# Gathering second-table expert rows into an idle weight ring, with two weight chunks loaded later

## Chip, cores and metric

One core of a Trainium2 chip runs the whole program: two transformer-like blocks on 256 tokens of width 1024, in f32. The metric is the time of one execution on the device in microseconds; smaller is better.

## What is computed

The part of the first block that the change touches is the expert layer (PEER). For every token, 8 heads choose 16 experts each out of 16384 (128 = 8 x 16 per token), and each expert is one row of a table `peer_u` and one row of a table `peer_v`:

```
def expert_chunk(args):
    xc, ic, gc = args
    u = jnp.take(u_tab, ic, axis=0)
    a = jnp.einsum('chkd,cd->chk', u, xc)
    wgt = gc * jax.nn.gelu(a)
    vv = jnp.take(v_tab, ic, axis=0)
    return jnp.einsum('chk,chkd->cd', wgt, vv)
```

Ahead of it stand attention, a short convolution and the projections that give the queries and scores; behind it stands the second block: its input projection `w_in_2` (parts u, q2, k2, v, o and gates), an S5 mixer, an mLSTM mixer, and a feed-forward part.

## The kernel before

The 256 tokens are two tiles of 128 (one token for each partition). For each tile the kernel goes through 128 experts (`e` counts both tiles, 0 to 255), and each is one step on five engines:

- POOL gathers, for every token, that token's row of `peer_u` (`gather_u`, L572) and of `peer_v` (`gather_v`, L586), with an indirect DMA of 128 rows x 1024 f32, 512 KB, each. The loop issues u(e+1) and then v(e), in this order.
- DVE multiplies the u row by the token's input and sums it (`dot_expert`, L2104), into one of 16 columns `dots`. Between the dots it does pieces of the routing of later heads.
- ACT takes the GELU, multiplies by the gate, and writes a diagonal matrix of these weights, one of 8 (`weigh_expert`, L1513, L1517, L1522).
- PE multiplies the diagonal by the v row and adds it up in PSUM over a tile's 128 experts (`sum_expert`, L975: four matmul instructions for each expert). Between the sums PE does other work that is ready: queries and scores of the first block, and, in the second tile, parts u and q2 of the second block's input projection for tile 0 (sums 172 to 194).

The rows land in the buffer `gathered` (G), twelve slots of 4 KB for each partition: five for u (`NU`), seven for v (`NV`). So u(e) waits until the dot of e-5 is done (semaphore `dot_ready`), and v(e) until the sum of e-7 is done (`expert_summed`). SP loads weights in chunks of 2 MB into a ring `weight_ring` of three slots (16 KB for each partition), in the order of `CHUNKS`; `SLOT`, `BEFORE` and `LAST_USE` give a chunk's slot, the chunk that held it, and the last group of matmuls that reads that one. During the expert phase the ring's slots hold the last query weights (read by PE until experts 27 and 36), a chunk of `ada_w` (read at expert 58), and the chunks u, q2 and k2 of `w_in_2`. PE first reads u at expert 172 and q2 at expert 188; k2 is loaded when 251 sums are done. Behind the chunk q2, SP waits for the scores and for `ada` 11, issues four small loads, and waits for those 251 sums.

## Time and profile before

| | |
|---|---|
| median of 3 runs | 1431.93 us (1430.23 to 1440.47) |
| span of the profiled execution | 1439.3 us |
| PE / DVE / ACT / POOL busy | 86% / 60% / 29% / 36% of the span |
| read from HBM | 395 MB, 275 GB/s over the span |
| gathers (software queue) | 271 MB |
| chain that ended last | PE 52%, DVE 12%, POOL 11%, issue 10%, DMA 8% |
| expert phase | first gather at 174 us, last sum ends at 944 us |

"Issue" is time in which an engine waited for nothing that the profile shows. A row of the profile gives for an engine how long it was busy and what ended the idle time ahead of it. The name behind the arrow is inferred from semaphore events: where the engine named had long been done, it was another ("remote" is one that the profile could not name).

### The profile page before, as it was taken

The page shows a single profiled execution, that of the slowest core. Times are in us where ns is not written, and L with a number is a line of the kernel's source. Part 1 is how long each engine was busy: PE and PEld are TensorE (multiplying, and loading weights), DVE is VectorE, ACT ScalarE, POOL GpSimd, SP SyncE. Part 2 cuts the span into 40 slices and gives each one's busy share as a digit, 9 for nine tenths or more (in the row PEclk, how much of TensorE's full clock was granted, in tenths as well). Part 3 has the DMA queues.
Part 4 walks back from the last instruction along what each step waited for, and adds up shares of the span by engine and source line. Part 5 has one row for each costly group of instructions (what it writes and reads, how often), then busy time and mean ns, then how long its engine had stood idle before and what let it go on. Part 6 is the DMA issues. An engine that isn't in the chain of part 4 may idle for free.

```text
span 1439.3 us, 14255 instructions
## 1 busy us (share of the span) xinstructions
PE 1237.8 (86%) x4539; PEld 652.8 (45%) x4539; DVE 861.5 (60%) x1726; ACT 421.1 (29%) x1126; POOL 518.3 (36%) x578
## 2 busy tenths in 40 slices
PE   7999976989877776777698767699999999999997
PEld 2676533645322222222344222275444444899443
DVE  2445577374564565667646657728999552577445
ACT  2213242333443242342333333332212511222000
POOL 1000165555666666666666756600111200000000
PEclk9999998999999999999898999999999999999999
DMA  9896599999999999999999999934343423444440
GB/s 348 306 331 240 203 360 324 401 348 374 361 406 363 346 377 364 369 371 365 353 344 344 387 366 344 376 132 169 128 148 117 161 88 120 173 176 176 175 175 30
DMA packets 130795, 397.32 MB, mean 276 GB/s; under 512 B 10381, under 2 KB 11789, under 8 KB 130464
## 3 DMA queue, kind: packets, MB, share of 16 engines
q0 software_dynamic: 74448, 271.09, 49.9%
q1 hardware_dynamic: 54404, 120.14, 23.0%
q10 hardware_dynamic: 1868, 5.18, 1.0%
q8 instruction: 37, 0.61, 0.2%
q14 instruction: 38, 0.30, 0.1%
HBM read 395.32 MB, written 1.05 MB: 275 GB/s over the span
## 4 chain that ended last, share of the span: by engine, by line
PE 52%; DVE 12%; POOL 11%; issue 10%; DMA 8%; DVEq 3%; another core or an unknown queue 2%; ACT 2%; ACTq 0%; POOLq 0%
PE psum L663 16%; PE psum L975 14%; PE psum L1259 6%; PE psum L1298 6%; POOL gathered L572 5%; POOL gathered L586 5%; DVE work L1759 4%; DMA gathered<-in_peer_v_dram,expert_idx 4%; DVE gathered L2104 3%; DMA gathered<-in_peer_u_dram,expert_idx 3%; DVE work L2393 2%; PE psum L771 1%; DMA weight_ring<-in_w_in_dram 1%; PE psum L690 1%
## 5 line engine op out<-in xcount | busy, mean ns | idle before, releaser
L975 PE MATMUL psum<-gathered,modr 128*128 128x512 f32 x1024 | 513.5, 638 | 169.7 <-issue 71.2
L2104 DVE CUSTOM_DVE_ANT_0 gathered<-gathered,psum 128x1024 f32<-128x1024 f32 x256 | 311.4, 1217 | 203.4 <-DMA gathered<-in_peer_u_dram,expert_idx 184.8
L975 PEld LDWEIGHTS psum<-gathered,modr 128*128 128x128 f32 x1024 | 188.5, 199 | 470.1 <-issue 321.5
L572 POOL DMA_INDIRECT gathered<-in_peer_u_dram,expert_idx x256 | 243.0, 949 | 254.4 <-DVE expert_idx L1767 166.8
L586 POOL DMA_INDIRECT gathered<-in_peer_v_dram,expert_idx x256 | 244.9, 957 | 182.6 <-PE psum L975 73.1
L663 PE MATMUL psum<-weight_ring,featT 128*128 128x512 f32 x384 | 170.5, 597 | 1.7 <-ACT featT L1350 1.7
L1513 ACT ACTIVATE gel<-dots 128x1 f32<-128x1 f32 x256 | 50.9, 199 | 264.6 <-DVEq L2106 132.6
L1759 DVE TENSOR_TENSOR work<-work 128x1088 f32<-128x1088 f32 (+4 forms) x107 | 100.0, 951 | 32.8 <-ACT work L1612 18.1
L663 PEld LDWEIGHTS psum<-weight_ring,featT 128*128 128x128 f32 x384 | 71.1, 190 | 91.1 <-issue 88.9
L663 PEld LDWEIGHTS psum<-featT,weight_ring 128*128 128x128 f32 x768 | 101.7, 193 | 20.8 <-issue 14.7
L663 PE MATMUL psum<-featT,weight_ring 128*128 128x128 f32 (+2 forms) x768 | 108.3, 297 | 3.1 <-ACT featT L1350 1.5
L1522 ACT ACTIVATE modr<-ident,wgt 128x128 f32<-128x128 f32 x256 | 102.8, 402 | 22.5 <-issue 4.5
L1517 ACT ACTIVATE wgt<-gel,expert_gate 128x1 f32<-128x1 f32 x256 | 75.4, 294 | 25.0 <-issue 8.0
L608 POOL TENSOR_TENSOR gathered<-gathered,vectors 128x2048 f32<-128x2048 f32 x3 | 15.4, 5121 | 81.3 <-ACT gathered L1377 81.3
L1350 ACT COPY featT<-psum 128x512 f32<-128x512 f32 (+1 forms) x28 | 14.7, 560 | 74.1 <-PE psum L639 60.1
L602 POOL TENSOR_TENSOR gathered<-gathered,vectors 16x1024 f32<-16x1024 f32 x1 | 3.0, 3036 | 91.0 <-ACT gathered L1638 91.0
L1759 DVE TENSOR_TENSOR gathered<-gathered,psum 128x256 f32<-128x256 f32 (+1 forms) x17 | 8.7, 513 | 36.7 <-PE psum L663 31.3
L663 PE MATMUL psum<-weight_ring,uT 128*128 128x512 f32 x64 | 29.9, 622 | 0.0
L1748 ACT ACTIVATE work<-work,pack 128x256 f32<-128x256 f32 x28 | 12.7, 500 | 56.8 <-DVE work L1759 56.8
L1377 ACT COPY gathered<-psum 128x512 f32<-128x512 f32 (+1 forms) x20 | 10.2, 520 | 65.1 <-PE psum L663 57.6
L663 PE MATMUL psum<-featT,gathered 128*128 128x256 f32 x128 | 29.0, 382 | 0.0
L1759 DVE TENSOR_TENSOR vectors<-weight_ring 128x1024 f32<-128x1024 f32 x14 | 16.5, 1220 | 20.9 <-PE psum L1298 20.9
(365 smaller groups left out, 1375.0 us busy)
## 6 DMA issues: line engine op xcount, KB each, us to landing
weight_ring<-in_w_in_dram SPq DMA_DIRECT2D x13, 2048.0 KB
weight_ring<-in_ada_w_dram SPq DMA_DIRECT2D x10, 2048.0 KB
weight_ring<-in_w_up_dram SPq DMA_DIRECT2D x8, 2048.0 KB
weight_ring<-in_w_down_dram SPq DMA_DIRECT2D x8, 2048.0 KB
weight_ring<-in_peer_wq_dram SPq DMA_DIRECT2D x3, 2048.0 KB
gathered<-in_ada_w_dram SPq DMA_DIRECT2D x2, 2048.0 KB
gathered<-in_w_in_dram SPq DMA_DIRECT2D x2, 2048.0 KB
gathered<-in_peer_u_dram,expert_idx POOLq DMA_INDIRECT x256
```

The costliest lines, as they stand in the source:

```text
L572: pool.indirect_dma_start(u_rows[:, slot, :], None, T["peer_u"], bass.IndirectOffsetOnAxis(ap=expert_idx[:, r % 2, k:k + 1], axis=0),).the ...
L586: pool.indirect_dma_start(v_rows[:, slot, :], None, T["peer_v"], bass.IndirectOffsetOnAxis(ap=expert_idx[:, r % 2, k:k + 1], axis=0),).the ...
L663: last = pe.matmul(psum[0:m, bank, 0:n], lhs(k), rhs(k), start=(k == 0), stop=(k == kt - 1))
L975: mm = pe.matmul(psum[:, SUM_BANK + half, :], diag[:, e % 8, :], v_rows[:, slot, 512 * half:512 * (half + 1)], start=(e % EXPERTS == 0), s ...
L1259: last = pe.matmul(psum[:, UP_BANKS * (n % 2) + bank, at:at + P], a(g, m), b(g), start=(g == 0), stop=(g == 3))
L1298: last = pe.matmul(psum[:, PRODUCT_BANK[i], :], a(g), b(g), start=(n == 0 and g == 0), stop=(n == WINOGRAD - 1 and g == 1))
L1513: act.activation(gel[:, col:col + 1], dots[:, col:col + 1], ACT.Gelu_apprx_tanh)
L1517: act.activation(wgt[:, col:col + 1], gel[:, col:col + 1], ACT.Copy, scale=expert_gate[:, r % 2, k:k + 1])
L1522: act.activation(diag[:, e % 8, :], ident[:, :], ACT.Copy, scale=wgt[:, col:col + 1]).then_inc(flag("diag_full"), 1)
L1759: return dve.tensor_tensor(o, a, b, op)
L2104: dve.tensor_tensor_reduce(u_rows[:, slot, :], u_rows[:, slot, :], h2_rows[t], 1.0, 0.0, ALU.mult, ALU.add, dots[:, col:col + 1])
L2393: dve.tensor_tensor_scan(z[:, i, :], r, z[:, i, :], 0.0, ALU.mult, ALU.add)
```

## The change

While the ring's slots stand empty, each holds four rows of v (4 x 4 KB = 16 KB). The table `SPILL` says for which experts a slot may be used, and `place_v` gives every v row the place that has been free longest. Slot 2 takes rows of experts 62 to 245, slots 1 and 0 of experts 62 to 145 (the last that uses slot 0 is 141). So there are 19 places for v rows from expert 62, 11 from 146, and 7 or 8 from 246: v(e) then waits for the sum of e-19, and from e = 157 of e-11. The first row in each place of the ring waits for the last matmuls that read the slot's weights. SP loads chunks u and q2 only when `SPILL_DONE` sums are done (146 and 142), and the four small loads now stand ahead of them. DVE's dot of expert e also waits until ACT has done the diagonal of e-16+1, because 16 columns of `dots` would otherwise be overwritten.

```
+SPILL = {2: (62, 246), 1: (62, 146), 0: (62, 146)}
+SPILL_LAST = {2: ("turn", ("ada", 11, 0)), 1: ("group", ("wqb", 7)), 0: ("group", ("wq", 11))}
+def place_v():
+    at, before, turn = [], [], []
+    last, uses = {}, {}
+    for e in range(TT * EXPERTS):
+        open_ = list(range(NV))
+        for r in sorted(SPILL):
+            lo, hi = SPILL[r]
+            if lo <= e < hi:
+                open_ += [NV + 4 * r + j for j in range(4)]
+        slot = min(open_, key=lambda k: (last.get(k, -1), k))
+        at.append(slot)
+        before.append(last.get(slot))
+        turn.append(uses.get(slot, 0))
+        last[slot], uses[slot] = e, uses.get(slot, 0) + 1
+    return at, before, turn
+V_AT, V_BEFORE, V_TURN = place_v()
+SPILL_DONE = {r: 1 + max(e for e in range(TT * EXPERTS) if (V_AT[e] - NV) // 4 == r) for r in SPILL}
...
-                if c == LAST_ADA + 3:
+                if c == LAST_ADA + 1:
                     turn_read_wait(sp, "sc", TT - 1, 3)
                     group_wait(sp, "ada", 11)
...
+                if c in (LAST_ADA + 1, LAST_ADA + 2):
+                    sp.wait_ge(flag("expert_summed"), SPILL_DONE[SLOT[c]])
+                if c == LAST_ADA + 3:
                     sp.wait_ge(flag("expert_summed"), TT * EXPERTS - LATE_LOAD)
...
-                r, k, slot = e // ROUTE, e % ROUTE, e % NV
-                if e >= NV:
-                    pool.wait_ge(flag("expert_summed"), e - NV + 1)
+                r, k, slot = e // ROUTE, e % ROUTE, V_AT[e]
+                if V_BEFORE[e] is not None:
+                    pool.wait_ge(flag("expert_summed"), V_BEFORE[e] + 1)
+                elif slot >= NV:
+                    kind, last = SPILL_LAST[(slot - NV) // 4]
+                    if kind == "turn":
+                        turn_wait(pool, *last)
+                    else:
+                        group_wait(pool, *last)
...
-                slot = e % NV
-                pe.wait_ge(v_full[slot], 16 * (e // NV + 1))
+                pe.wait_ge(v_full[V_AT[e]], 16 * (V_TURN[e] + 1))
...
+                if e >= TOPK:
+                    dve.wait_ge(flag("diag_full"), e - TOPK + 1)
```

On POOL's queue, around v62 (L586 is `gather_v` before, L627 after). Before:

```order
148 L586 DMA gathered<-in_peer_v_dram,expert_idx 128x1024 [waits expert_summed]
149 L572 DMA gathered<-in_peer_u_dram,expert_idx 128x1024 [waits dot_ready]
150 L586 DMA gathered<-in_peer_v_dram,expert_idx 128x1024 [waits expert_summed]
151 L572 DMA gathered<-in_peer_u_dram,expert_idx 128x1024 [waits dot_ready,idx_ready]
152 L586 DMA gathered<-in_peer_v_dram,expert_idx 128x1024 [waits expert_summed]
```

And after:

```order
148 L627 DMA gathered<-in_peer_v_dram,expert_idx 128x1024 [waits expert_summed]
149 L607 DMA gathered<-in_peer_u_dram,expert_idx 128x1024 [waits dot_ready]
150 L627 DMA weight_ring<-in_peer_v_dram,expert_idx 128x1024 [waits bank_full1]
151 L607 DMA gathered<-in_peer_u_dram,expert_idx 128x1024 [waits dot_ready,idx_ready]
152 L627 DMA weight_ring<-in_peer_v_dram,expert_idx 128x1024 [waits bank_full1]
```

The order of the gathers is the same; from v62 they go to the ring, and the first twelve there wait for groups of matmuls in place of sums.

On SP's queue, behind the last query weights (L513 is the load of a chunk before, L548 after; `w_in` rows are chunks u, q2 and k2 of the second block). Before:

```order
27 L513 DMA weight_ring<-in_ada_w_dram 128x8x512 [waits bank_full1]
28 L513 DMA weight_ring<-in_w_in_dram 128x8x512 [waits bank_full1] x2
29 L506 DMA vectors<-in_ln_g_dram 1x1024 [waits bank_full1,turn_read,turned]
30 L506 DMA vectors<-in_ln_b_dram 1x1024
31 L508 DMA work<-in_meta_tokens_dram 16x1024
32 L509 DMA work<-in_s_bc_dram 128x1024
33 L513 DMA weight_ring<-in_w_in_dram 128x8x512 [waits expert_summed]
34 L513 DMA weight_ring<-in_w_in_dram 128x8x512 [waits bank_full1]
```

And after:

```order
27 L548 DMA weight_ring<-in_ada_w_dram 128x8x512 [waits bank_full1]
28 L538 DMA vectors<-in_ln_g_dram 1x1024 [waits bank_full1,turn_read]
29 L538 DMA vectors<-in_ln_b_dram 1x1024
30 L540 DMA work<-in_meta_tokens_dram 16x1024
31 L541 DMA work<-in_s_bc_dram 128x1024
32 L548 DMA weight_ring<-in_w_in_dram 128x8x512 [waits expert_summed]
33 L548 DMA weight_ring<-in_w_in_dram 128x8x512 [waits expert_summed,bank_full1]
34 L548 DMA weight_ring<-in_w_in_dram 128x8x512 [waits expert_summed,turned]
```

The two chunks moved from ahead of the four small loads to behind them, and all three chunks now wait for sums.

## Rows read from the trace of the kernel before

**Rows 1.** The page's slices of the span: GB/s moved, 36 us each.
```profile
GB/s 348 306 331 240 203 360 324 401 348 374 361 406 363 346 377 364 369 371 365 353 344 344 387 366 344 376 132 169 128 148 117 161 88 120 173 176 176 175 175 30
```

**Rows 2.** Busy time by stretch: PE, PEld, DVE, ACT, POOL, clock, DMA share, GB/s.
```profile
372.00:925.00 553.00, 415.66 (x951) 163.11 (x949) 345.17 (x808) 200.71 (x623) 363.78 (x382) 0.94 0.96 366
...
540.00:558.00 18.00, 13.88 (x28) 4.74 (x28) 8.72 (x15) 6.29 (x21) 10.44 (x12) 1.00 1.02 408
558.00:562.00 4.00, 1.98 (x4) 0.68 (x4) 1.48 (x4) 1.80 (x6) 2.86 (x4) 1.00 0.60 185
...
613.00:643.00 30.00, 21.70 (x44) 7.89 (x42) 20.26 (x38) 10.42 (x34) 20.79 (x21) 0.94 0.97 362
```

**Rows 3.** Groups by line, 375 to 925 us: busy, mean ns | idle before, releasers.
```profile
L2104 DVE CUSTOM_DVE_ANT_0 gathered<-gathered,psum 128x1024 f32<-128x1024 f32 x192 | 233.7, 1217 | 140.2 <-DMA gathered<-in_peer_u_dram,expert_idx 123.3 <-issue 16.3
L586 POOL DMA_INDIRECT gathered<-in_peer_v_dram,expert_idx x190 | 182.3, 960 | 122.9 <-issue 47.4 <-PE psum L975 40.5 <-remote 34.9
L572 POOL DMA_INDIRECT gathered<-in_peer_u_dram,expert_idx x190 | 180.4, 950 | 66.0 <-issue 58.1 <-DVEq L2106 8.0
```

**Rows 4.** POOL's waits, 375 to 613 us: us in total, times, longest.
```profile
POOL gathered L586 <- PE psum L975: 16.0, 7, 4.4
POOL gathered L572 <- DVEq L2106: 7.7, 7, 2.8
POOL gathered L586 <- remote: 7.0, 2, 4.4
```

**Rows 5.** The same, 613 to 911 us.
```profile
POOL gathered L586 <- PE psum L975: 24.5, 16, 3.0
POOL gathered L586 <- remote: 24.1, 10, 4.8
```

**Rows 6.** POOL's timeline, six v gathers; then matmuls of L975 until 722.9 us.
```profile
723.14 0.94 POOL L586 DMA_INDIRECT gathered<-in_peer_v_dram,expert_idx  x1 [1.43 <-PE psum L975]
...
726.82 0.94 POOL L586 DMA_INDIRECT gathered<-in_peer_v_dram,expert_idx  x1 [1.50 <-PE psum L975]
...
732.22 0.94 POOL L586 DMA_INDIRECT gathered<-in_peer_v_dram,expert_idx  x1 [0.74 <-issue]
...
770.65 0.94 POOL L586 DMA_INDIRECT gathered<-in_peer_v_dram,expert_idx  x1 [1.49 <-PE psum L975]
...
774.38 0.94 POOL L586 DMA_INDIRECT gathered<-in_peer_v_dram,expert_idx  x1 [1.55 <-PE psum L975]
...
780.32 0.94 POOL L586 DMA_INDIRECT gathered<-in_peer_v_dram,expert_idx  x1 [1.28 <-PE psum L975]
...
190.00:722.90 532.90, 353.74 (x708) 129.65 (x708) 0.94 0.97 366
```

**Rows 7.** POOL's timeline: v82, v94, u127 and v126 (start, duration, idle before).
```profile
432.12 1.33 POOL L586 DMA_INDIRECT gathered<-in_peer_v_dram,expert_idx  x1 [4.11 <-PE psum L975]
...
466.41 0.94 POOL L586 DMA_INDIRECT gathered<-in_peer_v_dram,expert_idx  x1 [4.41 <-remote]
...
552.86 0.94 POOL L572 DMA_INDIRECT gathered<-in_peer_u_dram,expert_idx  x1 [0.30 <-issue]
558.23 0.94 POOL L586 DMA_INDIRECT gathered<-in_peer_v_dram,expert_idx  x1 [4.43 <-PE psum L975]
```

**Rows 8.** Instructions of one line: L975's matmuls, then L586's gathers.
```profile
190.00:545.10 355.10, 233.93 (x480) 86.76 (x480) 0.95 0.97 367
...
170.00:558.10 388.10, 119.57 (x126) 0.96 0.97 367
```

**Rows 9.** SP's queue, chunks u and q2.
```profile
309.48 0.99 SPq L513 DMA_DIRECT2D weight_ring<-in_w_in_dram  x2
```

**Rows 10.** Busy time of the stretch in which they load, columns as in group 2.
```profile
309.00:341.00 32.00, 26.16 (x85) 15.42 (x83) 14.13 (x31) 10.62 (x30) 16.15 (x18) 0.89 1.02 391
```

**Rows 11.** PE's timeline, the two sums with idle time ahead there.
```profile
320.49 3.75 PE L975 MATMUL psum<-gathered,modr 128*128 128x512 f32 x4 [4.10 <-ACT modr L1522]
...
341.99 3.24 PE L975 MATMUL psum<-gathered,modr 128*128 128x512 f32 x7 [2.72 <-ACT modr L1522]
```

**Rows 12.** Timeline around 582 us: DVE behind dot 131, POOL at u136.
```profile
581.72 0.87 DVE L2041 MAX8 work<-work 128x8 f32<-128x128 f32 x4 [6.10 <-issue]
...
581.90 0.94 POOL L572 DMA_INDIRECT gathered<-in_peer_u_dram,expert_idx  x1 [2.87 <-issue]
```

More of the change, by code:

```diff
@@ L308, in build, with v_row @@
         rows = G[:, :].rearrange("p (s n) -> p s n", s=NU + NV)
-        u_rows, v_rows = rows[:, 0:NU, :], rows[:, NU:NU + NV, :]
+        u_rows = rows[:, 0:NU, :]
+        def v_row(e):
+            k = V_AT[e]
+            if k < NV:
+                return rows[:, NU + k, :]
+            return ring[:, (k - NV) // 4, D * ((k - NV) % 4):D * ((k - NV) % 4 + 1)]
         h2_rows = [psum[:, b:b + 2, :].rearrange("p b n -> p (b n)") for b in H2_BANK]
@@ L371, in build @@
         u_full = [sem(f"u_full{i}") for i in range(NU)]
-        v_full = [sem(f"v_full{i}") for i in range(NV)]
+        v_full = [sem(f"v_full{i}") for i in range(NV + 4 * RING)]
         S_ = {}
@@ L586, in gather_v @@
                 pool.indirect_dma_start(
-                    v_rows[:, slot, :], None, T["peer_v"],
+                    v_row(e), None, T["peer_v"],
                     bass.IndirectOffsetOnAxis(ap=expert_idx[:, r % 2, k:k + 1], axis=0),
```

2 lines of the change are left out of this document (1 added, 1 removed).

## Prediction

> **What bounds the kernel now.** I read the page's rows of slices first, then the groups of instructions from 375 to 925 us, then the waits of POOL there, and last its timeline beside PE's. The diff touches only the expert phase (first gather at 174 us, last sum at 944 us) and, in it, mostly experts 62 to 255. Between the two the slices show 324 to 406 GB/s [rows 1]: 256 experts fetch two tiles of 512 KB (1.05 MB for each expert). From 372 to 925 us the mean is 366 GB/s; in stretches where nothing stops, 408 GB/s (540 to 558 us), right after a stop of POOL 185 GB/s [rows 2]. So the transfers are near their limit but not at it: 553 us at 366 GB/s would be 496 us at 408.
>
> PE isn't the bound: 28 matmuls, seven experts, take 18 us from 540 to 558 us, 2.57 us each, with PE busy 13.9 of 18 us [rows 2]. DVE (234 us of 550) and ACT have room too. POOL starts a pair of gathers every 2.5 us (950 and 960 ns, and 0.3 us after each) when nothing holds it [rows 3]; that is 419 GB/s, about what the transfers manage. But 190 pairs took 550 us, 2.89 us each. The difference is waits of POOL in front of **v** gathers: from 375 to 613 us 16.0 + 7.0 us in 9 waits, of which 20.3 us are above the usual 0.3; waits in front of u gathers behind DVE are 7.7 us [rows 4]. From 613 to 911 us it is 24.5 + 24.1 us in 26 waits, 40.8 us above the usual [rows 5]. These are the waits the change is about, since v(e) waits for the sum of e-7, and afterwards of e-19 or e-11.
>
> They are of two kinds. *Slot waits*: v183 starts at 723.14 us; the 708th matmul, that is the sum of expert 176, ended 0.3 us before it. Six are like that (v183, 184, 186, 199, 200, 202), where PE is behind because it also computes u and q2 of tile 0; they come to 8.0 us, 6.2 above the usual [rows 6]. *Late waits*, the rest: v126 sat 4.43 us after u127 and started at 558.23 us [rows 7]. It needs 120 sums. At 545.1 us 480 matmuls had ended, 120 sums, and at 558.1 us 126 v gathers were out [rows 8]: the sum was done 13 us before. The count seems to reach POOL late, and in every such case the wait ends just as the gather issued two before it has landed, when the transfers have run nearly dry. I infer that from the trace; a wait on something of the gather queue itself would look alike.
>
> **The change, part by part.**
> 1. *Slot waits, -6 us (0 to -6.2).* From v157 on a row waits for the sum of e-11: four more experts, 10 us of PE's lag, against waits of 0.7 to 1.6 us each [rows 6]. They go. What is late next is PE itself, which has 0.6 us spare in every expert (13.9 of 18 us), so it catches up before the phase ends.
> 2. *Late waits, -14 us (0 to -55).* 20.3 us between 375 and 613 us, and 40.8 less 5.8 (the five slot waits that this view puts under PE) = 35.0 us behind, 55 us in all. Below: if they belong to the gather queue, none goes. Above: all. Between: if the count is late and comes through only once the transfers run dry, the stop isn't avoided, it is put off by the extra slots, 12 x 2.5 = 30 us up to v156 and 4 x 2.5 = 10 us behind. Late waits now come up to 34 us apart (v82 at 432.12 and v94 at 466.41 us, twelve experts apart [rows 7]). With 64 and 44 us between them, 20.3 x (1 - 34/64) = 9.5 and 35.0 x (1 - 34/44) = 8.0 go, 17.5 in all; 3 of it I take back, as longer full stretches run at 2.57 and not at 2.5 us an expert. I take this middle value since all the waits of one piece are alike in length (about 4.4 us, what the queue needs to empty), which a count that is late by itself wouldn't give.
> 3. *The two chunks, +10 us where they land, -4 where they leave.* Now SP issues u and q2, 2 MB each, at 309.48 us [rows 9], in a stretch where transfers run at 391 GB/s and PE is busy 26.2 of 32 us [rows 10]. PE idles 4.10 and 2.72 us for diag columns there, whose rows came late [rows 11]; 6.8 us is the most that comes back, 0 the least, and I take 4. Afterwards they wait for sums 146 and 142, about 613 us. There the transfers already carry 362 GB/s and PE is busy 21.7 of 30 us [rows 2], so 4.19 MB at 408 GB/s cost 10.3 us, less if they fill the holes after POOL's stops (7), more if u gathers are late enough to stop DVE (16). PE wants u at expert 172, 26 experts or 65 us later, so the load itself isn't waited for. The four small loads (ln0, meta, bc) keep their place in time: they wait for ada 11 either way.
> 4. *SP and POOL otherwise.* SP has nothing between the small loads and k2's at expert 251, so what queues behind its new waits is only k2, which waits longer. POOL's first rows in the ring wait for matmul groups of experts 27, 36 and 58, over by then. 0 us.
> 5. *DVE's new wait for diag_full(e-15)*, one for each dot: ACT would have to be 15 experts behind. The longest hold of this kind that I found, DVE 6.10 us without work, is two or three experts [rows 12]. 0 us, at most 0.05 us of issue an expert, hidden by the wait for u rows.
>
> Sum: -6 - 14 - 4 + 10 = -14 us on the profiled 1439.3 us, 1425 us. The median of the runs is 1431.93 us, 7.4 us below the profiled span, so the time is 1418 us.
>
> **A rule against it.** Full stretches reach 408 GB/s for 18 us [rows 2]. The Trainium skill (DMA: Bandwidth & Descriptors, "Where 436 GB/s comes from") says that between HBM and SBUF a core's share of HBM binds, at about 358 GB/s. By that rule 366 GB/s is already the end, nothing of the waits would come back, and the chunks would cost nothing or 10 us: the third case below. Its time is worked out from rows; the trace disagrees with the rule's figure here.
>
> **Rivals.**
> - *All late waits go.* If the count is late by some 13 us and then comes by itself, both new depths cover it. 55 + 6 us of waits are gone, and the transfers become the bound: 190 pairs at 2.57 us are 488 us, and 8 us of holds on DVE stay, 496 for 550 us: -54. With +10 and -4, -48: 1384 us. For it: only v gathers wait so, never u gathers, which speaks against the queue. Against: the even length.
> - *None goes, no change.* The stops belong to the gathers, or move to the u side, which keeps five slots: DVE held 6.10 us made u136 wait 2.87 us [rows 12]. Then -6 + 10 - 4 = 0, and up to +2 as not all slot waits leave: 1433 us.
> - *Slower.* While the chunks load, gathers get some 260 of 390 GB/s (12.5 MB moved from 309 to 341 us, 4.2 of them the chunks) [rows 10]. If that comes on full stretches and u rows, five deep, stall DVE, the loss is 16 us; if the late stops also move to u, nothing pays for it: +16, about 1447 us. It decides as soon as the load costs more than slot and late waits give, 20 us with all of it.
>
> **How the numbers follow.** Thinned late waits (1418, its own range 1408 to 1428): 0.37. All gone (1384): 0.23. None gone (1433): 0.28. Slower (1447): 0.12. The range leaves out the far ends: 1386 to 1440 us. Within 1%, about what a measurement of this kernel can tell from no change, is 1417.6 to 1446.3 us. Faster by over 1%: the second case and more than half of the first, with its lower half and what lies between the two, 0.47. Slower by over 1%: 0.09. Same: 0.44.
>
> **What would show it.** In the profile after: v gathers 183 to 202 without waits behind a sum just ended (step 1). POOL's waits before v gathers from 375 to 911 us: 60 us now; about 40 says put off, near 0 says gone, and u waits that grow say moved. GB/s from 375 to 613 us: 370 now; 380 for the first case, 400 for the second. SP's two loads near 600 us with gathers thinner for 30 us behind them (step 3). Wrong altogether if PE starts to wait for u's chunk at expert 172, or if DVE stands for diag_full.

## The result, and the profile after

The changed kernel takes 1468.82 us (median of 5 runs, 1459.07 to 1470.34) against 1438.72 us for the kernel before on the same chip (5 runs, 1430.23 to 1446.6). The ratio is 1.0208, with a 95% interval from 1.0168 to 1.0248: **slower by 2.1%**. I had forecast 1418 us, 14 us faster. The time lies outside the range, and above the 1447 us of the rival that ended on the other side. A second set of runs, further down, gave 1.0141 (1.0096 to 1.0186). The profiled execution of the changed kernel has a span of 1457.3 us, 18.0 us over that of before. In the changed file L607 and L627 are the u and v gathers, L1015 the sums, L2146 the dot product with L2148 the drain that carries its count, and L1562 the diagonal that ACT writes.

The slices of the page, as [rows 1]:

```profile
GB/s 346 304 329 231 220 367 319 403 308 329 373 398 360 357 288 339 230 372 391 409 373 352 334 371 363 369 177 231 116 116 173 137 109 116 174 174 174 173 173 30
```

Two slices of 36 us have dropped deeply, the 15th (288, before 377) and the 17th (230, before 369). The stretches of [rows 4] and [rows 5] and the two places inside, columns as in [rows 2]; first the changed kernel:

```profile
375.00:613.00 238.00, 167.49 (x319) 65.54 (x316) 128.37 (x320) 69.82 (x234) 142.00 (x150) 0.81 0.87 331
613.00:911.00 298.00, 223.21 (x552) 99.32 (x551) 184.21 (x431) 105.90 (x337) 192.97 (x204) 0.89 0.98 372
525.00:550.00 25.00, 19.07 (x29) 6.88 (x29) 2.47 (x5) 10.61 (x31) 5.64 (x6) 0.72 0.46 178
575.00:600.00 25.00, 14.81 (x29) 5.95 (x30) 4.81 (x16) 6.71 (x25) 6.57 (x7) 0.80 0.58 224
```

and the kernel before:

```profile
375.00:613.00 238.00, 177.71 (x370) 63.16 (x369) 145.49 (x358) 85.67 (x264) 158.27 (x167) 0.96 0.97 371
613.00:911.00 298.00, 225.76 (x556) 95.16 (x554) 187.49 (x435) 109.29 (x340) 194.99 (x205) 0.93 0.96 361
```

All of the loss is ahead of 613 us: 40 GB/s less for 238 us are 9.5 MB, 23 us at the 408 GB/s of [rows 2]. From 525 to 550 us POOL issued 6 gathers and DVE ran 5 instructions, while PE and ACT went on. Behind 613 us the changed kernel moves more than before, but 4.2 MB of it are the two chunks. Expert by expert: v64 starts 3.0 us earlier than before, v112 2.9 us, v120 11.1 us later, v136 21.5 us later, and from there on the distance stays between 20 and 27 us. The last sum ends 17.5 us later (961.6 against 944.1 us).

POOL's waits, 375 to 613 us, as [rows 4]:

```profile
POOL gathered L607 <- DVEq L2148: 38.3, 11, 16.1
...
POOL weight_ring L627 <- remote: 7.1, 4, 3.6
POOL gathered L627 <- PE psum L1015: 5.4, 3, 2.7
POOL weight_ring L627 <- PE psum L1015: 2.8, 2, 2.5
POOL gathered L627 <- remote: 2.5, 1, 2.5
```

In front of v gathers 17.8 us are left of 23.0. In front of **u** gathers 38.3 us stand where 7.7 us stood. Taken over 375 to 960 us and above the usual 0.3 us, v waits fell from 65.0 to 43.5 us and u waits rose from 8.1 to 53.9 us. Two waits make up 28.7 us of the 53.9, one at u121 and one at u135 (POOL's timeline):

```profile
549.06 0.94 POOL L607 DMA_INDIRECT gathered<-in_peer_u_dram,expert_idx  x1 [16.05 <-DVEq L2148]
...
600.86 0.94 POOL L607 DMA_INDIRECT gathered<-in_peer_u_dram,expert_idx  x1 [12.67 <-DVEq L2148]
```

A u gather needs the place of the dot product five experts back, so DVE stood. DVE's timeline says for whom, once for ACT's exponential of the routing scores, once for the read of the finished sum of tile 0, which wants all 128 sums:

```profile
547.41 0.19 DVE L2129 TENSOR_REDUCE work<-work 128x2 f32<-128x32 f32 x1 [23.15 <-ACT work L1518]
...
598.14 1.29 DVE L1799 TENSOR_TENSOR modr<-psum,modr 128x512 f32<-128x512 f32 x2 [19.83 <-PE psum L1015]
```

DVE had come to these two points at 524 and 578 us. ACT and PE were far behind: at the start of v104 PE was 12 experts behind the v gathers (before: 5), at v112 and v120 13 (before: 3). ACT's timeline shows where it lost them, first in front of diagonals:

```profile
427.78 0.40 ACT L1562 ACTIVATE modr<-ident,wgt 128x128 f32<-128x128 f32 x1 [1.19 <-PE psum L1015]
434.84 0.40 ACT L1562 ACTIVATE modr<-ident,wgt 128x128 f32<-128x128 f32 x1 [6.20 <-remote]
444.63 0.40 ACT L1562 ACTIVATE modr<-ident,wgt 128x128 f32<-128x128 f32 x1 [8.94 <-remote]
```

PE's timeline over the same 18 us has exactly one sum (four matmuls; of the last only the first falls into the window) behind each of them:

```profile
428.33 1.96 PE L1015 MATMUL psum<-gathered,modr 128*128 128x512 f32 x4 [1.43 <-issue]
435.38 3.75 PE L1015 MATMUL psum<-gathered,modr 128*128 128x512 f32 x4 [5.10 <-issue]
445.18 1.19 PE L1015 MATMUL psum<-gathered,modr 128*128 128x512 f32 x1 [6.04 <-issue]
```

PE has summed each expert as soon as its diagonal was there. ACT waits only for the sum *eight* experts before, which by these rows is long done. The diagonal written at 444.63 us waited 8.94 us for a sum that had ended at 409.24 us, 35 us earlier. It is the increment of the count itself that comes late, not ACT that looks late: the trace also keeps the times at which the semaphore changed, and these are 422.74, 427.76, 434.82 and 444.61 us, each about 0.02 us ahead of the one diagonal that it releases, for sums that had all ended between 404.1 and 409.2 us. This is the late count of the prediction, but now ACT meets it. Behind 500 us ACT meets it three times more, when it copies the sums of a layer norm that PE computes with L1058 (the fourth copy is in time):

```profile
506.89 0.59 ACT L1390 COPY vectors<-psum 128x512 f32<-128x512 f32 x1 [4.15 <-remote]
520.23 0.59 ACT L1390 COPY vectors<-psum 128x512 f32<-128x512 f32 x1 [10.89 <-remote]
532.88 0.59 ACT L1390 COPY vectors<-psum 128x512 f32<-128x512 f32 x1 [10.20 <-remote]
540.34 0.59 ACT L1390 COPY vectors<-psum 128x512 f32<-128x512 f32 x1 [5.01 <-PE psum L1058]
```

```profile
512.12 1.12 PE L1058 MATMUL psum<-vectors,ones 1*128 1x512 f32 x2
...
525.58 1.12 PE L1058 MATMUL psum<-vectors,ones 1*128 1x512 f32 x2
...
538.23 2.07 PE L1058 MATMUL psum<-vectors,ones 1*128 1x512 f32 x2
```

(ACT's timeline, then PE's.) The fourth copy starts 0.04 us behind PE's matmuls; that is what a count takes when nothing holds it. The second and third start 7.0 and 6.2 us behind; for the first, the matmuls had ended at 500.8 us.

Over the whole phase ACT's waits by releaser (375 to 960 us; L1581 reads the products of u and q2):

```profile
ACT modr L1562 <- remote: 61.1, 11, 9.6
...
ACT modr L1562 <- PE psum L1015: 30.3, 9, 5.0
ACT modr L1581 <- remote: 26.1, 2, 20.6
ACT vectors L1390 <- remote: 25.2, 3, 10.9
```

Counting every wait over 0.5 us in front of a diagonal, whatever the view puts it under, it is 108.8 us; in the kernel before 3.5 us. The other two rows are not new in kind: in the kernel before ACT had 18.6 us under the same reads of products and 12.1 us under the layer-norm copies.

Two more things belong to the two stops of DVE. Late counts also fell inside them: in the second (578.3 to 598.1 us) ACT's diagonals came only at 582.09 and 587.02 us, after waits of 9.64 and 4.07 us, so 8.7 of its 19.8 us passed before PE could sum the last six experts of the tile in 10.5 us. And PE's granted clock is lower than before, 0.81 against 0.96 from 375 to 613 us. It fell to the lower of its two levels (1.2 GHz) at 433.4 us, while PE stood for 5.10 us, and the sum behind that, at 435.38 us, took 3.75 us; the one at 428.33 us, at the upper level (2.4 GHz), took 1.96 us. In the first stop the mean clock was 0.67 (1.00 in the same stretch of the kernel before), in the last 8 us of the second 1.00:

```profile
524.00:547.40 23.40, 17.47 (x24) 5.81 (x24) 0.19 (x1) 8.22 (x25) 5.48 (x6) 0.67 0.53 208
590.00:598.00 8.00, 8.00 (x19) 3.23 (x17) 0.00 (x0) 3.35 (x13) 0.00 (x0) 1.00 0.09 35
```

So the lower clock has a part in the first stop, as a result of PE's waits; no run separates how large it is.

### The profile page after: what moved, and what is told of

Its sections match the earlier page's. It is cut to its first block, busy times and chain, and to the rows that moved or that the text cites. A ratio compares the mean times of both kernels' runs of the same rounds, so it can differ in the third digit from the quotient of the medians.

```text
span 1457.3 us, 14496 instructions
## 1 busy us (share of the span) xinstructions
PE 1245.7 (85%) x4539; PEld 669.3 (46%) x4539; DVE 861.4 (59%) x1726; ACT 414.4 (28%) x1126; POOL 520.0 (36%) x578
## 4 chain that ended last, share of the span: by engine, by line
PE 57%; DVE 10%; issue 10%; DMA 6%; another core or an unknown queue 6%; DVEq 3%; ACT 3%; POOL 3%; ACTq 0%; POOLq 0%; SPq 0%
PE psum L1015 19%; PE psum L704 17%; PE psum L1299 6%; PE psum L1338 6%; DVE work L1799 3%; DMA gathered<-in_peer_u_dram,expert_idx 2%; DMA weight_ring<-in_w_in_dram 2%; DVE gathered L2146 2%; DVE work L2435 1%; PE psum L812 1%; POOL gathered L607 1%; PE psum L731 1%; ACT modr L1562 1%; DMA gathered<-in_peer_v_dram,expert_idx 1%
## 5 line engine op out<-in xcount | busy, mean ns | idle before, releaser
L1015 PE MATMUL psum<-gathered,modr 128*128 128x512 f32 x652 | 333.1, 657 | 93.0 <-issue 54.5
L2146 DVE CUSTOM_DVE_ANT_0 gathered<-gathered,psum 128x1024 f32<-128x1024 f32 x256 | 311.3, 1216 | 159.5 <-DMA gathered<-in_peer_u_dram,expert_idx 126.2
L607 POOL DMA_INDIRECT gathered<-in_peer_u_dram,expert_idx x256 | 244.6, 955 | 302.2 <-DVE expert_idx L1807 167.0
L1015 PE MATMUL psum<-weight_ring,modr 128*128 128x512 f32 x372 | 190.3, 663 | 77.4 <-issue 53.1
L1015 PEld LDWEIGHTS psum<-gathered,modr 128*128 128x128 f32 x652 | 127.7, 206 | 275.2 <-issue 254.8
L627 POOL DMA_INDIRECT gathered<-in_peer_v_dram,expert_idx x163 | 155.8, 956 | 102.2 <-issue 44.3
L1015 PEld LDWEIGHTS psum<-weight_ring,modr 128*128 128x128 f32 x372 | 75.5, 211 | 188.0 <-issue 183.6
L1562 ACT ACTIVATE modr<-ident,wgt 128x128 f32<-128x128 f32 x256 | 102.8, 402 | 125.5 <-remote 61.1
L1799 DVE TENSOR_TENSOR work<-work 128x1088 f32<-128x1088 f32 (+4 forms) x107 | 100.0, 952 | 38.3 <-ACT work L1652 22.6
L704 PE MATMUL psum<-featT,weight_ring 128*128 128x128 f32 (+2 forms) x768 | 111.5, 304 | 5.7 <-DMA weight_ring<-in_w_in_dram 3.3
L704 PEld LDWEIGHTS psum<-featT,weight_ring 128*128 128x128 f32 x768 | 105.0, 198 | 22.6 <-issue 13.9
L627 POOL DMA_INDIRECT weight_ring<-in_peer_v_dram,expert_idx x93 | 88.7, 953 | 53.1 <-issue 25.7
L1799 DVE TENSOR_TENSOR gathered<-gathered,psum 128x256 f32<-128x256 f32 (+1 forms) x17 | 8.7, 513 | 36.4 <-PE psum L704 31.1
L1390 ACT COPY vectors<-psum 128x512 f32<-128x512 f32 x14 | 8.2, 585 | 73.3 <-PE psum L731 27.6
```

Of the source, the lines that this page charges most:

```text
L607: pool.indirect_dma_start(u_rows[:, slot, :], None, T["peer_u"], bass.IndirectOffsetOnAxis(ap=expert_idx[:, r % 2, k:k + 1], axis=0),).the ...
L627: pool.indirect_dma_start(v_row(e), None, T["peer_v"], bass.IndirectOffsetOnAxis(ap=expert_idx[:, r % 2, k:k + 1], axis=0),).then_inc(v_fu ...
L704: last = pe.matmul(psum[0:m, bank, 0:n], lhs(k), rhs(k), start=(k == 0), stop=(k == kt - 1))
L1015: mm = pe.matmul(psum[:, SUM_BANK + half, :], diag[:, e % 8, :], v_row(e)[:, 512 * half:512 * (half + 1)], start=(e % EXPERTS == 0), stop= ...
L1390: ins = act.activation(dst, src, func, **kw) if func else act.copy(dst, src)
L1562: act.activation(diag[:, e % 8, :], ident[:, :], ACT.Copy, scale=wgt[:, col:col + 1]).then_inc(flag("diag_full"), 1)
```

## The experiments

**Theory 1**, formed from this: counts of finished work, PE's above all, reach other engines late while transfers are saturated. With 7 places POOL is the first to run into one, stands about 4 us, and everybody catches up. With 19 places POOL runs on, ACT and DVE run into them, and DVE pays at the two points where it must wait for ACT and PE to come all the way up. **Rivals:** the chunks moved to 667 us (1), DVE's new wait (2), and lateness that belongs to the gathers' queue (3). As misses came in, theories 4 to 6 replaced part of this. All ratios are to the kernel before on the same chip.

**One part alone: late chunks, a third of the places, DVE's wait.**

```
x1:  before, with  sp.wait_ge(flag("expert_summed"), 146 or 142)  ahead of chunks u and q2
x2:  -SPILL = {2: (62, 246), 1: (62, 146), 0: (62, 146)}
     +SPILL = {2: (62, 246)}                 # and the chunks where they were
x3:  before, with  dve.wait_ge(flag("diag_full"), e - TOPK + 1)  ahead of the dot product
```

> The kernel before with one part of the change alone: the chunks u and q2 of the second tile are loaded after the sums of experts 145 and 141 instead of at 309 us, and SP's small loads go ahead of them; the v rows keep their 7 places. Theory 1 (counts of finished sums reach the other engines late while the gathers saturate the transfers, and the added places for rows move the stop from POOL, where it is cheap, to ACT, PE and DVE): the places are the cause, the chunks are not; about 3 us come off ahead of 376 us as in the changed kernel, and 3 to 8 us are paid back where the two loads of 2 MB fall between the gathers. Ratio to the kernel before 0.997 to 1.006. Rival 1 (the moved chunks are what made the changed kernel slower): 1.012 to 1.02.

> The changed kernel with the ring's third slot alone lent to v rows (11 places from expert 62 to 245), the chunks u and q2 loaded at about 309 us as in the kernel before; DVE's added wait stays. Theory 1: ACT writes a diagonal only when the sum of 8 experts before has been counted, so with 11 places it is already ACT and not POOL that stops first. ACT's waits for counts grow, PE falls more than 8 experts behind the v gathers, and the ratio is 1.005 to 1.02, though only a third of the places was added and no chunk was moved. Rival 1 (chunks): 0.99 to 1.0. Rival 3 (lateness belongs to the gather queue; more places simply give POOL more room): 0.985 to 1.0.

> The kernel before with nothing added but DVE's wait ahead of each dot product until ACT has written the diagonal of 16 experts before. Theory 1: that diagonal is 8 or more experts old whenever DVE comes to it, so 0.998 to 1.003. Rival 2 (this wait holds DVE, and so the u gathers): 1.01 or more, and the waits of POOL ahead of u gathers behind DVE rise from 8 us in 375 to 960 us towards 59 us.

Measured: late chunks 1.0043 (1.0016 to 1.0071), 11 places with early chunks 1.0047 (1.0014 to 1.0081), DVE's wait 1.0019 (0.9983 to 1.0054). So rival 1 as the whole cause and rival 2 fall: 0.4% is 6 us of the 30. The 11 places came out just under the lower edge of what theory 1 gave (1.005), and above what rivals 1 and 3 gave. ACT has four waits over 2.5 us in front of diagonals there, 19 us together (the changed kernel: 19, 103 us), DVE's longest wait for the sums is 9.1 us and POOL's longest behind DVE 6.6 us. That is the same picture, smaller. The parts do not add up to 2.1%, and stops as long as the two stand only where 19 places do.

**Fewer gathers in flight.** v(e) also waits until the row of e-2 (x6) or e-3 (x10) has landed, from expert 24 on:

```
+                if e >= 24:
+                    pool.wait_ge(v_full[(e - 2) % NV], 16 * ((e - 2) // NV + 1))
```

> The kernel before, with POOL waiting from expert 24 on, ahead of v(e), until the v row gather of e-2 has landed: two experts, 2.1 MB, are the most that is outstanding, so the transfers can't be fed beyond what they deliver. Theory 1: the late counts belong to the backlog of transfers; with a small backlog counts come in time, POOL's stops of 3 to 5 us every dozen experts and ACT's waits of 4 us and more vanish, each replaced by short waits for a landing; by time 0.975 to 1.005. Rival 3 (lateness belongs to the number of gathers issued or to something else than the backlog): the long waits stay and the short ones come on top, 1.01 to 1.04.

> As the run with the pace of two, but v(e) waits for the landing of the row of e-3, so one expert more (3 instead of 2) can be outstanding. With the pace of two the late counts were gone (no wait of ACT in front of a diagonal) but the transfers fell from 365 to 330 GB/s. Theory 1: lateness grows with the backlog; at three the transfers run at 350 to 400 GB/s, and a few late counts come back or none: 0.98 to 1.01. If late counts had nothing to do with the backlog, all of POOL's long v waits (20 to 40 us under PE and unknown releasers) would be here again and the ratio 1.0 to 1.03.

Measured: 1.0456 (1.0399 to 1.0514) and 1.0051 (1.0027 to 1.0074). The pace of two is slower than theory 1 had said (1.005 at most), since the transfers drop to 329 GB/s, but it ends the late counts altogether, and with them every wait of ACT in front of a diagonal (3.5 us before, 0 here). DVE's drain shows it most plainly. It carries the count of a dot product; its row gives count, then shortest, median and longest duration in ns. From 375 to 911 us, kernel before, changed kernel, pace of two:

```profile
L2106 DVEq DRAIN  x187: 1181/1244/8144, 374.0 to 910.4; - x187
```

```profile
L2148 DVEq DRAIN  x176: 1181/1246/9615, 375.5 to 910.7; - x176
```

```profile
L2108 DVEq DRAIN  x167: 1181/1244/1319, 375.0 to 908.1; - x167
```

So it isn't PE's counts alone that are held up. DVE's are too, as I read these rows, up to 8.1 and 9.6 us against 1.24; the dot products ahead of the drains are no longer than before (1216 ns on average, against 1217). At the pace of three the wait for a landing hardly ever bound (2.0 us in 2 waits), POOL's waits for counts were there as before (47.4 and 27.4 us up to 911 us), and the longest drain was 7.3 us. This pace was nearly no change at all and proves little.

**Half the bytes.** The v gathers fetch only columns 0 to 511 of a row:

```
-                    v_rows[:, slot, :], None, T["peer_v"],
+                    v_rows[:, slot, 0:D // 2], None, T["peer_v"],
```

> The kernel before with v gathers that fetch only the first 512 columns of a row (256 KB instead of 512 KB); PE multiplies these columns for both halves, so the second half of each v row is left out of the computation. The count of gathers and every wait stay as they are. 0.79 MB an expert at POOL's 2.5 us is 315 GB/s, below the 408 GB/s the transfers manage. Theory 1: no backlog, no late counts; POOL's waits of 3 us and more for counts vanish and the gathers go at POOL's own 2.5 us an expert: ratio 0.95 to 0.97. Rival 3 (lateness belongs to the number of gathers): the stops every dozen experts stay as long as they are, 0.98 to 1.0.

> The changed kernel with the same halved v gathers (second half of each v row left out). Theory 1: without a backlog the two kernels run alike, since neither 7 nor 19 places are ever short: ratio to the kernel before 0.95 to 0.975, within 5 us of the halved kernel before, and ACT's waits in front of diagonals fall from 108.8 us to a few. Rival 1 (chunks) or rival 2 (DVE's wait): 15 us or more above the halved kernel before.

Measured: 1.0005 (0.9973 to 1.0036) for the kernel before, 1.0146 (1.0089 to 1.0203) for the changed one. For both this was a plain miss of theory 1; for the kernel before it is what rival 3 had given (0.98 to 1.0, with the stops left as they are). The halved kernel before moves 280 GB/s where it moved 371,

```profile
375.00:613.00 238.00, 174.97 (x356) 65.23 (x355) 148.10 (x362) 87.37 (x273) 158.86 (x169) 0.93 0.84 280
```

and POOL waits in front of v gathers as before (375 to 911 us, as [rows 4] and [rows 5] added up: 51.6 and 34.6 us against 40.5 and 31.1):

```profile
POOL gathered L586 <- PE psum L975: 51.6, 30, 7.6
...
POOL gathered L586 <- remote: 34.6, 15, 4.7
```

Nor do the stops of the kernel before end because its transfers run dry. By the trace's packets, rows came at 349 to 411 GB/s over each of its 18 stops over 2.3 us, and still at 325 to 412 in the last microsecond before POOL went on. The lateness is not one of bytes, and **saturated transfers are not its cause**. Nor is it the amount in flight. Counted from the same packets, as rows issued and not yet landed from 375 to 911 us, and in units of one expert's two rows, the halved kernel before has 0.8 experts in flight on average and 1.9 at most, the pace of two 0.9 and 1.8; the one is late and the other is not. What does differ is POOL's step from one v gather to the next: its median is 2.50 us in the halved kernel and 2.48 in the kernel before, but 3.17 us at the pace of two. The halved changed kernel has its 110.7 us of waits in front of diagonals and its DVE waits of 23.9 and 14.3 us all the same, which shows the second half of theory 1 (who meets the late count) without the first.

**Sixteen diagonals in the changed kernel.**

```
-                if e >= 8:
-                    act.wait_ge(flag("expert_summed"), e - 7)
-                act.activation(diag[:, e % 8, :], ident[:, :], ACT.Copy,
+                if diag_before(e) is not None:          # e - 16 from expert 88 on
+                    act.wait_ge(flag("expert_summed"), diag_before(e) + 1)
+                act.activation(diag_of(e), ident[:, :], ACT.Copy,
```

> The changed kernel with 16 places for ACT's diagonals from expert 72 on (a second eight in the part of hbuf that the query transposes have left), so ACT waits for the sum of 16 experts before, no longer 8. Theory 1: ACT's waits in front of diagonals (108.8 us in the changed kernel) go nearly away, PE's lag behind the v gathers falls from 9 to 13 experts to fewer; what is left are the other readers of late counts (ACT's reads of the layer-norm sums, DVE behind ACT's exponential, DVE's read of the finished sum, POOL behind DVE). Ratio to the kernel before 1.003 to 1.015, so a third to four fifths of the loss come back. Rival 1 (the chunks at 667 us): no change, 1.018 to 1.024, the lag stays where it began, near expert 72. Rival 3: POOL's own waits, no change either, 1.018 to 1.024.

Measured: 1.0158 (1.0114 to 1.0202), just beyond what theory 1 gave and short of nothing gained. ACT's waits in front of diagonals went from 108.8 to 8.8 us, and yet the time lies between the two measurements of the changed kernel (1.0141 and 1.0208). ACT now loses its time at the next place, the copies of the layer-norm sums (44.8 and 26.6 us, the longest 23.5 and 24.0), DVE still stands 15.6 us for ACT's exponential and 18.4 us for the sums, and POOL's timeline has the same two stops at the same two experts:

```profile
542.56 0.94 POOL L624 DMA_INDIRECT gathered<-in_peer_u_dram,expert_idx  x1 [14.97 <-DVEq L2165]
...
592.84 0.94 POOL L624 DMA_INDIRECT gathered<-in_peer_u_dram,expert_idx  x1 [15.71 <-DVEq L2165]
```

So the 108.8 us in front of diagonals were not the price. The price is these two stops, and any reader of a late count on ACT's or PE's way leads to them.

**A pause on POOL.** The pace of two also gave POOL about 0.5 us more between gathers, so I tried the pause without the wait (theory 4), first with a drain:

```
+                if e >= 24:
+                    pool.memset(pause[:, 0:256], 0.0)      # x13: one column
+                    pool.drain()
```

> The kernel before, with POOL writing zeros into a tile of its own (128x256) and draining after each v gather from expert 24 on: a pause of about 0.4 to 0.6 us an expert that waits for nobody. The halved rows showed that the late counts are not a matter of bytes (POOL stopped as often at 270 GB/s as at 365), and the pace of two showed that they vanish when POOL pauses by some 0.5 us in each expert: DVE's drain that carries its count took 1.24 us every time there, and up to 8 us in the kernel before. Theory 4 (counts of other engines are held up while POOL issues gather after gather with 0.3 us between; a pause in each expert lets them through): POOL's stops of 3 to 5 us vanish, DVE's drains are 1.24 us again; 2.5 + 0.5 = 3.0 us an expert against 2.89 now gives 1.00 to 1.02. Theory 1 (it was the backlog of gathers not yet landed that the pace of two bounded): the stops and long drains stay until the backlog is gone; since 3.0 us an expert is slower than the transfers' 2.6, they vanish here too, but no earlier than the backlog does. If neither holds, stops stay and the pause comes on top: 1.03 to 1.06.

> The changed kernel with the same pause in each expert from 24 on. Theory 4: the more places did harm only because POOL, no longer stopped by a full ring of v rows, never pauses, so that the late counts fell on ACT and DVE. With a pause in every expert ACT's waits in front of diagonals fall from 108.8 us to under 10, DVE's two long waits (23 and 20 us) go, and the changed kernel comes within 0.5% of the kernel before with the same pause: ratio 0.995 to 1.015. Rival 1 or 2 (chunks, DVE's wait) or a fixed cost of the added places: 15 us or more above that kernel.

> The kernel before with the shortest pause: POOL writes one column of zeros and drains after each v gather from expert 24 on, about 0.1 to 0.3 us an expert. Theory 4: a size between nothing and the pause above; if the pause itself is what lets counts through and 0.2 us is enough, POOL goes at 2.7 us an expert instead of 2.89 on average: 0.975 to 0.99. If it needs longer pauses, stops become rarer but do not vanish: 0.995 to 1.01.

Measured: 1.6944 (1.6844 to 1.7044), 1.6929 (1.6829 to 1.703) and 1.6916 (1.6816 to 1.7017). This measured something else. With one column of zeros, POOL's timeline:

```profile
404.19 0.11 POOL L599 MEMSET pause<- 128x1 f32 x1
408.99 0.94 POOL L573 DMA_INDIRECT gathered<-in_peer_u_dram,expert_idx  x1 [4.69 <-issue]
```

A drain behind gathers holds POOL some 5 us, whatever was written (POOL's idle time ahead of the next u gather has a median of 4.76, 4.78 and 4.97 us in the three runs). The transfers fall to 145 GB/s. No count is late there (DVE's drains take 1246 ns at most) and both kernels take the same time, but it settles nothing between the theories, since both pause and empty queue are there at once.

Then without a drain, the zeros into two places in turn:

```
+                    for i in range(n * (e - 24), n * (e - 23)):      # n = 1; x18: 3
+                        if i >= 2:
+                            pool.wait_ge(flag("paused"), i - 1)
+                        pool.memset(pause[:, i % 2, :], 0.0).then_inc(flag("paused"), 1)
```

> The kernel before, with POOL writing zeros once (128x128) into a tile of its own after each v gather from expert 24 on, without a drain: in the runs with a drain POOL stood 4.8 us in front of each next gather, so these measured the drain. A write of 128x128 took POOL 0.20 us at the kernel's start. Theory 4 (counts are held up while POOL issues gathers with no more than 0.3 us between): POOL at 2.7 to 3.0 us an expert, DVE's counting drains nearer to 1.24 us each, fewer stops of 3 to 5 us; ratio 0.98 to 1.01. Theory 5 (counts are late when more than about four gathers are in flight, whatever POOL does between; the pace of two bounded just this): stops and long drains stay as long as the gathers in flight reach six; the small pause only shifts them, 0.995 to 1.015.

> The changed kernel with the same write of zeros in each expert from 24 on. Theory 4: ACT's waits in front of diagonals fall from 108.8 us to under 50, and the ratio to the kernel before from 1.02 to 1.00 to 1.012. Theory 5: the changed kernel keeps most of its loss, 1.015 to 1.03, since nothing bounds what is in flight.

> The same with three writes an expert, so that POOL needs about 3.0 to 3.2 us an expert and the transfers (2.6 us an expert at 408 GB/s) always catch up with it: few gathers in flight and a pause in each expert at once, reached without any wait for a landing. Both theories 4 and 5 expect no stop of more than 2 us and DVE's drains at 1.24 us, at 1.02 to 1.06. If stops and long drains are here too, it is the wait for a landing itself that did it in the run with the pace of two, and neither theory holds.

Measured: 1.0004 (0.9989 to 1.0018), 1.0052 (1.0032 to 1.0073) and 1.0421 (1.039 to 1.0452). The surprise stood beside them: on this chip the **kernel before took 1366.07 us**, 5% less than on any chip so far. Nothing is late in any of the three, though with one write up to 3.2 experts are in flight there, more than the kernel before ever had on a late chip (2.5). The kernel before with one write from 375 to 613 us moves 409 GB/s, and its longest drain is 2.3 us:

```profile
375.00:613.00 238.00, 186.93 (x376) 64.37 (x376) 166.75 (x376) 96.86 (x294) 193.22 (x274) 0.99 1.03 409
```

```profile
L2112 DVEq DRAIN  x189: 1183/1244/2256, 374.0 to 863.8; - x189
```

Whether that was the pause or the chip (theory 6) the next three had to tell: the changed kernel again, and the two kernels with one write a second time.

> The changed kernel as it is, a second time. The last three runs fell on a chip where the kernel before takes 1366 us and not 1438 to 1447, its gathers run at 409 GB/s without a stop and DVE's counting drains take 1.24 us. Theory 6 (whether counts are held up is a property of the chip, or of what else goes on beside it, not of the kernel; the change only decides who waits for them): where the kernel before takes about 1440 us this run shows ratio 1.014 to 1.025 again, with ACT's waits in front of diagonals at 100 us; where it takes about 1366 us the transfers alone set the pace in both, ACT does not wait, and the ratio is 0.997 to 1.008 (nothing gained from the places, some us paid for chunks among the gathers).

> The kernel before with one write of zeros on POOL in each expert, as before. On a chip where counts are held up (kernel before about 1440 us) theory 4 expects DVE's drains at 1.24 us, no stops over 2 us and a ratio of 0.95 to 0.99; theory 5 and theory 6 expect stops and long drains as in the kernel before, 0.995 to 1.01. On a chip like the last, 0.998 to 1.002 again.

> The changed kernel with one write of zeros in each expert. Where counts are held up: theory 4, at or under the kernel before, 0.95 to 1.0; theories 5 and 6, as the changed kernel without it, 1.014 to 1.025. On a chip like the last, 1.003 to 1.008 again, and the changed kernel without the writes the same within 0.2%.

They fell on a chip where the kernel before takes 1445.67 us. Measured: 1.0141 (1.0096 to 1.0186), 1.0028 (1.0004 to 1.0052), 1.0146 (1.0083 to 1.0209). The same kernel before with one write, stretch and drain as above, on this chip:

```profile
375.00:613.00 238.00, 180.92 (x373) 66.10 (x371) 145.80 (x357) 85.42 (x267) 175.34 (x250) 0.94 0.97 367
```

```profile
L2112 DVEq DRAIN  x183: 1183/1244/6924, 374.5 to 909.7; - x183
```

One and the same program, 409 GB/s and punctual there, 367 GB/s and late here. This pause does nothing, but it was a short one: one write moved POOL's median step from 2.48 to 2.57 us only, and the three writes (2.86 us) ran on the quick chip alone, so theory 4 falls for this size and is open for a longer one. Theory 5, more than about four gathers in flight, falls: 6.3 are in flight at most where nothing is late, 3.9 at most in the halved kernel before, which is late. The chip, or what goes on beside the kernel on it, decides (theory 6). The changed kernel has its two stops again, 15.95 us at u121 and 17.53 us at u135.

**The change without the running ahead.** The changed kernel complete, but with POOL's old wait:

```
-                if V_BEFORE[e] is not None:
-                    pool.wait_ge(flag("expert_summed"), V_BEFORE[e] + 1)
+                if e >= NV:
+                    pool.wait_ge(flag("expert_summed"), e - NV + 1)
```

> The changed kernel in every point (rows in 19 and 11 places, part of them in the weight ring, chunks late, DVE's wait) but with POOL's old wait in front of v(e): it waits for the sum of e-7, as in the kernel before, though its place has been free for longer. So the added places lie where they lie and are used, but can't let POOL run further ahead. Theory 6 (the loss is that late counts now stop ACT and DVE, eight and more experts back, no longer POOL): on a chip where the kernel before takes about 1440 us ACT's waits in front of diagonals fall from 100 us to under 10, DVE's two long waits go, and what is left is what the late chunks cost alone, ratio 1.001 to 1.008. Rival (rows in the ring, or the chunks together with them, cost by themselves): 1.012 to 1.025. On a chip where the kernel before takes 1366 us both expect 1.003 to 1.008.

Measured: 1.004 (1.0024 to 1.0055), on a chip where the kernel before takes 1367.26 us. There both theories had expected this, so the run decides nothing about the 2.1%. It does say that where nothing is late the change costs 6 to 7 us with the running ahead (the 1.0052 above, against 1.0004 for the kernel before with the same writes) and 5 to 6 us without it. That is about what the late chunks cost alone (1.0043, on a late chip).

## Why the prediction was wrong, step by step

*Step 2, the late waits, is the step that failed.* Its first half held. Counts are late, the added places put POOL's stops off, and its v waits fell by 21 us (I had -14 for the late ones and -6 for the slot waits). But I asked only whom a late count stops on **POOL**, the engine whose wait is edited. ACT reads the same count with eight places, and PE's other counts with none to spare, and neither had shown a long wait in front of a diagonal only because POOL had always stood first. What the change removed was a cheap stop of 2.4 to 4.8 us that kept every engine within seven experts of the others. What came instead were PE and ACT 12 to 13 experts behind, and the lag, with the late counts that fell inside, charged to DVE at its next two meeting points, 23.2 and 19.8 us. The five u rows covered some 7 us of each, so POOL stood 16.1 and 12.7 us. The answer to "where does the stall go" was missing: the prediction says what is late next only for PE.

Two readings under this step were wrong, and both could be seen in the kernel before. "Only v gathers wait so, never u gathers" isn't so: u104 and u136 waited 2.84 and 2.87 us for a count of DVE, whose drains behind these dot products took 8.14 us (at 481.65 us) and 7.92 us (at 573.72 us). The second is the 6.10 us without work of [rows 12], which I took for a hold of DVE's own. And the waits are not alike in length: the 18 over 2.3 us last from 2.4 to 4.8 us. This evenness was my reason for the middle value.

In the same step I read that the stops end when transfers have run nearly dry. Fewer gathers are in flight then (0.2 to 3.1, against 2.3 to 5.2 when the stop begins), but rows still come at full rate, and halved rows, with even less in flight, leave the stops as they are. The 185 GB/s behind a stop [rows 2] are what POOL's pause leaves, not what lets the count through.

*Step 1, the slot waits, -6 us.* They did not go. v201 and v202 waited 2.79 and 2.55 us, v184, 186 and 200 1.9 to 2.6 us. For v186 and v201 the sum had just ended (0.3 and 0.5 us before they started), as a slot wait has it; for v202, v184 and v200 it had ended 1.6, 3.3 and 9.9 us before, so these were late counts again. PE was 10 experts behind v184 and v200 instead of 6, so eleven places were no more room than seven had been. "They go" failed: the step took PE's lag to be what it was before.

*Step 3, the chunks, +10 and -4 us.* Right in both sizes, as can be seen where nothing else disturbs it. In the pair with one write on the quick chip, v64 starts at 354.8 against 357.5 us and the sum of expert 64 ends 4.0 us earlier. Then v144 starts 5.3 us earlier and v164 4.1 us later: 9.4 us, for chunks issued at 575.7 us. In the changed kernel of the first measurement they went out later than I said:

```profile
667.53 1.01 SPq L548 DMA_DIRECT2D weight_ring<-in_w_in_dram  x2
```

The last sum they wait for, that of expert 145, ended at 642.3 us, so this count was late as well, by 25 us.

*Step 4* held but for such delays: k2's load went out 4.6 us after its sum, that of expert 250, and PE stood 2.99 us for it. *Step 5, DVE's wait,* is 0 as said (1.0019, with 1 inside the interval).

*The rivals.* "None goes, the stops move to the u side" saw the right place, and its price of 6.10 us held on DVE was read from the only such row there was [rows 12]; at 13 experts of lag it is 23. "Slower" had the right sign with the wrong mechanism: chunks on full stretches cost 0.4%, not 16 us. "All late waits go" at 1384 us is what the kernel *before* does by itself on two chips, 1366 and 1367 us.

*The rule against it.* The Trainium skill (DMA: Bandwidth & Descriptors, "Where 436 GB/s comes from") puts the bound at about 358 GB/s, a stack's 716 GB/s divided by two cores. On a quick chip the kernel before with one write holds 409 GB/s over 238 us, and the kernel before 371 on a late one; for this program, which runs on one core, the measurement decides against the figure. The rule did not help to see the outcome: the transfers moved less, and not for want of bandwidth.

*What stays open.* What holds the counts up on some chips, and why the pace of two ends it, I can't say. Bytes, the amount in flight and a pause of 0.1 us are excluded; POOL's step is not, since no run on a late chip made it longer by more than 0.1 us without also waiting for a landing or draining. Each chip was used for one set of runs only, so the chip and what went on beside it at that time are not separated. That the added places cost nothing beyond the running ahead is shown only where no count is late; the run meant to show it where counts are late fell on a quick chip. That DVE's two waits carry the 2.1% rests on five profiles of late chips in which they stand at the same two experts, and on their absence in the runs at 1.005 and below (the longest stand of DVE at one of them there is 9.1 us, with 11 places); they were not removed by themselves.

## What to carry to other kernels

Before you deepen a ring, list every engine that waits for the same count and how many steps each has in hand; the shallowest wait behind the one you remove takes over, and if an engine has a point where it must wait for another to come all the way up, it pays for the new lag there. A short stop that keeps engines together can be worth more than it costs. And when a wait ends long after the work it waits for, run the same program on several chips before reasoning about it, since here the chip moved the time by 5% and the change by 2%.

## What was not expected of the hardware

- The kernel before took 1438 to 1447 us in five of the seven sets of runs (four chips and that of the first comparison) and 1366 to 1367 us in two, on two other chips. In what was profiled on the two (both kernels with one write, the changed one with POOL's old wait), counts came at once and the gathers ran at 408 or 409 GB/s without a stop. On the others a count took up to 35 us from the end of the sum to the engine that waits for it, against 0.04 us when nothing holds it.
- It is not PE alone: DVE's drain with a count took up to 8.1 us (changed kernel 9.6) where 1.24 us is its usual length.
- Late counts did not depend on bytes (280 or 371 GB/s) nor on the amount in flight (late with at most 1.9 experts in flight, at once with 3.2). They were gone when POOL waited for landings and its median step from one v gather to the next was 3.17 us in place of 2.48.
- A drain on POOL behind gathers held it some 5 us each time, and made the kernel 1.69 times as long.
